# The first stage takes its 17 tiles in an interleaved order, and the tiles that are put aside share four slots

## The chip, the cores and the metric

One core of a Trainium2 chip runs the whole program. The time is the device time of one execution in microseconds; the median of several runs is compared.

## The reference, cut to what matters

One decoder layer over a prompt of 2064 rows (16 learned tokens and 2048 of the prompt) and eight single-row samples. Every row is normalised and projected through one combined matrix; an indexer scores the keys and each query keeps the best 256:

```python
xn = rmsnorm(xp, norm_g[l])
u, gc, q, k, v, ga, iq, ik, iw = project(xn, w_in[l])
...
s = jnp.einsum('bthd,bsd->bths', iq.astype(jnp.float32), ik_all.astype(jnp.float32))
score = jnp.einsum('bth,bths->bts', iw.astype(jnp.float32), jax.nn.relu(s))
_, idx = lax.top_k(score, topk)
...
xp = xp + merge(cy, gc, o, ga, w_out[l])
```

The outputs include k, v and ik of every row. Each matrix product of the prompt is made of three in the kernel, with each operand split into a high part (xh, wh) and a low part (xl, wl).

## The kernel before, in words

The rows are cut into 17 tiles of 128. Four stages follow one another, with a barrier between them. The change lies in the first, `project_norm_and_keys` (line 160), and in one helper table above it.

For each tile the first stage loads x (512 KB, into one of three places of `xst`), squares it on ACT (line 304), makes the reciprocal root on POOL (lines 294 and 296), scales it on DVE (line 337), transposes it on PE (line 369), and splits the result: ACT copies the high part into `mem.xh` (line 318), and DVE subtracts to get the low part in `mem.xl` (line 347). PE then projects k, v, ik and iw from it (24 matmuls, line 377), ACT copies them to `natst` (lines 322 to 325), and SP writes them out (lines 239 to 241). PE transposes ik (line 384) for the indexer.

The normalised tiles are needed again by the second stage. There are only nine slots for them on the chip, so tiles 0 to 7 (slots 0 to 7) are written to DRAM, 2 x 512 KB each (lines 260 and 261, here called the spill of a tile), and tiles 8 to 16 stay in slots 0 to 8. The second stage first works on tiles 8 to 16 and reads the eight others back later, by their tile numbers.

Each engine has a list of its own, written out by hand. On PE, ACT and DVE it is the list of jobs: for each i, "xT" of i + 1 (transpose and split), "nat" of i (projection), "ikT" of i - 1. On ACT, ahead of xT of i, comes the square of tile i + 2. DVE scales tile i + 1 ahead of the low part of i. SP, which issues all DMAs of the stage, runs through rounds i = 0 to 17, and in round i it issues:

```python
for i in range(NT + 1):
    if i < NT:
        if i + XS < NT:
            load_x(i + XS)
        if i < HALF:
            sp.wait_ge(dve_job, J.count(J.jobs.index(("xT", i)) + 1, ("xT", "ikT")))
            ...
        if i < LAST:
            load_pages(sp, range(2 * i, 2 * i + 2), ptab, t.cache_idx_k, "o s d -> (o s) d", ikp, pages_in)
    if i:
        write_natural(i - 1)
```

XS is 3. The load of x waits until the tile three places earlier is scaled; the spill waits for the low part of tile i; the two index pages of a round each need a register load from `ptab` (line 156) and a DMA (line 157); the three writes of tile i - 1 wait for its copy on ACT. SP goes strictly in this order, so that a wait holds back all that follows. Round 8 also loads eight small pieces of constants (line 270), and round 14 the first two weight chunks of the second stage (line 149). ACT waits for the spill of tile i - 8 before it overwrites its slot with tile i (line 317); the last tile has a free slot.

Of the kernel before, what the change touches and what calls it, by code (L numbers as in the profile page):

```python
# [6 lines left out]
f32 = mybir.dt.float32  # L7
# [3 lines left out]
ALU = mybir.AluOpType  # L11
ACT = mybir.ActivationFunctionType
# [7 lines left out]
P = 128  # L20
NT = -(-LP // P)
LAST = NT - 1
LREM = LP - LAST * P
SROW, NS = 32, 8
# [3 lines left out]
IH = 4  # L28
# [128 lines left out]
        eng.dma_start(dst[:, n, :], cache[0, bass.ds(v, 1)].rearrange(layout)).then_inc(pages_in, 16)  # L157


def project_norm_and_keys(nc, t, mem):  # L160


# [11 lines left out]
    with ExitStack() as ctx:  # L174
# [24 lines left out]
        nat_done = sem("nat_done")  # L199
        spill = [sem(f"x_spill{s}") for s in range(HALF)]  # L200
        nat_out = [sem(f"nat_out{s}") for s in range(2)]
        n_in = [len(tile_rows(i)) for i in range(NT)]
        ptab = sb("ptab", [1, NS * NPAGE], i32)
        ptab_in, pages_in = sem("ptab_in"), sem("pages_in")
        ikp = index_pages(mem)
# [6 lines left out]
            eng.wait_ge(nat_out[i % 2], 16 * n)  # L212

        def slot(i):
            return i if i < HALF else i - HALF
        block = ctx.enter_context(nc.Block())

        @block.sync
        def _(sp):
            def load_x(i):  # L220
                if i >= XS:
                    sp.wait_ge(xs_done, i - XS + 1)
                if i == LAST:
                    sp.wait_ge(zeroed, 1)
                for p0, n, what, r0 in tile_rows(i):
                    src = {"meta": t.meta_tokens, "x": t.x_prompt[0], "sample": t.x_sample[:, 0, :]}[what]
                    sp.dma_start(xst[p0:p0 + n, i % XS, :], src[r0:r0 + n, :]).then_inc(x_in[i % XS], 16)

            def write_natural(i):

                sp.wait_ge(nat_done, i + 1)
                n = natst[:, i % 2]
                for p0, rows, what in ([(0, P, "p")] if i < LAST else [(0, LREM, "p"), (SROW, NS, "s")]):
                    r = slice(i * P, i * P + rows)
                    ko = t.nk_p[0, 0, r] if what == "p" else t.nk_s[0, :, 0]
                    vo = t.nv_p[0, 0, r] if what == "p" else t.nv_s[0, :, 0]
                    io = t.nik_p[0, 0, r] if what == "p" else t.nik_s[0, :, 0]
                    q = slice(p0, p0 + rows)
                    sp.dma_start(ko.rearrange("t n d -> t (n d)"), n[q, 0:128]).then_inc(nat_out[i % 2], 16)
                    sp.dma_start(vo.rearrange("t n d -> t (n d)"), n[q, 128:256]).then_inc(nat_out[i % 2], 16)  # L240
                    sp.dma_start(io, n[q, 256:320]).then_inc(nat_out[i % 2], 16)
            load_x(0)
            sp.dma_start(gb[:, :], t.norm_g[0].unsqueeze(0).to_broadcast([128, D])).then_inc(g_in, 16)
            load_x(1)
            sp.dma_start(mem.cst[:, :], t.consts[:, 0:NCONST]).then_inc(c_in, 16)
            w3 = t.w_in[0].rearrange("(c p) n -> p c n", p=128)
            sp.dma_start(wn[:, :, 0:256], w3[:, :, OFF["k"]:OFF["k"] + 256]).then_inc(w_in_s, 16)
            sp.dma_start(wn[:, :, 256:NAT], w3[:, :, OFF["ik"]:OFF["ik"] + 68]).then_inc(w_in_s, 16)
            load_x(2)
            sp.dma_start(bcb[:, :], t.consts[0:32, NCONST:NCONST + BANDX]).then_inc(bias_in, 16)  # L250
            sp.dma_start(relb[:, :], t.rel_bias).then_inc(bias_in, 16)
            sp.dma_start(ptab[:, :], t.page_table.rearrange("b n -> (b n)").unsqueeze(0)).then_inc(ptab_in, 16)
            sp.wait_ge(ptab_in, 16)
            for i in range(NT + 1):
                if i < NT:
                    if i + XS < NT:
                        load_x(i + XS)
                    if i < HALF:
                        sp.wait_ge(dve_job, J.count(J.jobs.index(("xT", i)) + 1, ("xT", "ikT")))
                        sp.dma_start(t.d_xh[i], mem.xh[:, slot(i)].rearrange("p c t -> p (c t)").bitcast(f32)).then_inc(spill[i], 16)  # L260
                        sp.dma_start(t.d_xl[i], mem.xl[:, slot(i)].rearrange("p c t -> p (c t)").bitcast(f32)).then_inc(spill[i], 16)
                    if i < LAST:
                        load_pages(sp, range(2 * i, 2 * i + 2), ptab, t.cache_idx_k, "o s d -> (o s) d", ikp, pages_in)
                if i:
                    write_natural(i - 1)
                if i == HALF:

                    for dst, src in ((mem.lg, t.conv_ln_g), (mem.lb, t.conv_ln_b)):
                        for q in range(NQ):
                            sp.dma_start(dst[QA * q:QA * q + QA, :], src[0, P * q:P * q + P].rearrange("(g a) -> a g", a=QA),  # L270
                                         allow_slow_non_contiguous=True).then_inc(ln_in, 16)
                if i == LAST - 2:
                    for n in range(2):
                        load_weights(sp, t, mem, n)
            sp.wait_ge(ln_in, 16 * 2 * NQ)
            nat_written(sp, LAST)
            nat_written(sp, LAST - 1)
            sp.wait_ge(pages_in, 16 * NS * NPAGE)
            for s in range(HALF):
                sp.wait_ge(spill[s], 32)  # L280
# [17 lines left out]
        @block.scalar  # L298
        def _(act):
            def square(i):  # L300
                x_arrived(act, i)
                if i:
                    act.wait_ge(sq_done, i)
                nc.scalar.activation(sq[:, :], xst[:, i % XS, :], ACT.Square, accum_out=ssq[:, i:i + 1]).then_inc(sq_done, 1)
            square(0)
            square(1)
            act.wait_ge(w_in_s, 32)
            nc.scalar.activation(wnh[:, :, :], wn[:, :, :], ACT.Copy).then_inc(w_hi, 1)
            for n, (kind, i) in enumerate(J.jobs):
                if kind == "xT" and i + 2 < NT:  # L310
                    square(i + 2)
                act.wait_ge(pe_job, n + 1)
                u = psum[:, n % 4]
                if kind == "xT":
                    if i >= HALF:
                        if i < 2 * HALF:
                            act.wait_ge(spill[i - HALF], 32)
                    nc.scalar.activation(mem.xh[:, slot(i)].rearrange("p c t -> p (c t)"), u, ACT.Copy).then_inc(act_job, 1)
                elif kind == "nat":
                    if i >= 2:  # L320
                        nat_written(act, i - 2)
                    nc.scalar.activation(natst[:, i % 2, 0:256], u[:, 0:256], ACT.Copy)
                    nc.scalar.activation(natst[:, i % 2, 256:384].rearrange("p (a d) -> p a d", a=2),
                                         u[:, 256:320].unsqueeze(1).to_broadcast([128, 2, 64]), ACT.Copy).then_inc(nat_done, 1)
                    nc.scalar.activation(mem.iw[:, i], u[:, 320:324], ACT.Copy, scale=float(IH) ** -0.5).then_inc(act_job, 1)
                elif kind == "bias":
                    nc.scalar.activation(rrow[:, :], u[0:NH, 0:BANDX], ACT.Copy).then_inc(act_job, 1)
                else:
                    nc.scalar.activation(mem.ikh[:, i * P:(i + 1) * P], u[:, 0:128], ACT.Copy).then_inc(act_job, 1)

        @block.vector
        def _(dve):
# [7 lines left out]
            scale(0)  # L340
            for n, (kind, i) in enumerate(J.jobs):
                u = psum[:, n % 4]
                if kind == "xT":
                    if i + 1 < NT:
                        scale(i + 1)
                    dve.wait_ge(act_job, n + 1)
                    nc.vector.tensor_tensor(out=mem.xl[:, slot(i)].rearrange("p c t -> p (c t)"), in0=u,
                                            in1=mem.xh[:, slot(i)].rearrange("p c t -> p (c t)").bitcast(f32),
                                            op=ALU.subtract).then_inc(dve_job, 1)
                elif kind == "ikT":  # L350
                    dve.wait_ge(act_job, n + 1)
                    nc.vector.tensor_tensor(out=mem.ikl[:, i * P:(i + 1) * P], in0=u[:, 0:128],
                                            in1=mem.ikh[:, i * P:(i + 1) * P].bitcast(f32), op=ALU.subtract).then_inc(dve_job, 1)

        @block.tensor
        def _(pe):
            ident = part(mem.cst, "ident")
            for n, (kind, i) in enumerate(J.jobs):
# [11 lines left out]
                elif kind == "nat":  # L370
                    if i == 0:
                        pe.wait_ge(w_lo, 1)
                    pe.wait_ge(dve_job, J.count(J.jobs.index(("xT", i)) + 1, ("xT", "ikT")))
                    xh, xl = mem.xh[:, slot(i)], mem.xl[:, slot(i)]
                    for c in range(KC):
                        for k, (a, b) in enumerate(((xh, wnh), (xh, wnl), (xl, wnh))):
                            last = nc.tensor.matmul(u[:, 0:NAT], a[:, c, :], b[:, c, :], start=(c == 0 and k == 0),
# [1778 lines left out]
```

## Time and profile before

| what | value |
|---|---|
| runs | median 1750.65 us of 3 (1749.55 to 1751.58) |
| the profiled execution | 1748.58 us, span 1746.9 us |
| PE busy in the span | 1521.4 us (87%) |
| DVE | 1026.1 us (59%) |
| ACT | 722.6 us (41%) |
| POOL | 485.6 us (28%) |
| first stage | from the start to 122.35 us, where the second stage's first work starts |

Engines: PE is TensorE (PEld its weight loads), DVE VectorE, ACT ScalarE, POOL GpSimd, SP SyncE; SPq is SP's queue of issued DMAs. Times in the rows are microseconds from the start of the span. The stage is 7% of the span, so what it does is read from windows of its own time and not from the shares above.

### The profile page before, as it was taken

What the parts mean: (1) busy time and instruction counts of PE and PEld (TensorE: products, weight loads), DVE (VectorE), ACT (ScalarE), POOL (GpSimd) and SP (SyncE); (2) the same over time, 40 slices, a digit from 0 to 9 for tenths busy, and PEclk for the clock granted to TensorE, in tenths of its full rate; (3) what the DMA queues carried; (4) which work ended last, traced back from release to release, by engine and by line L of the source; (5) the groups of instructions that cost most, each with busy time, mean ns of one, the idle gap of its engine ahead of it and who ended that gap; (6) DMA issues with size and microseconds to landing.
All of it is one profiled execution on the core that took longest, in us unless ns stands there. A gap on an engine that the chain in (4) does not pass through costs nothing. (4 is left out here: it accounts for less than half of the span.)

```text
span 1746.9 us, 28490 instructions
## 1 busy us (share of the span) xinstructions
PE 1521.4 (87%) x10637; PEld 1298.9 (74%) x10637; DVE 1026.1 (59%) x2135; ACT 722.6 (41%) x1302; POOL 485.6 (28%) x334
## 2 busy tenths in 40 slices
PE   5698979979989799995489999999998887559998
PEld 5686979969989679995366777776666666448886
DVE  2333989879998798888224434455545555334332
ACT  4345413253222442221115555556556554355441
POOL 2120314613437412353321011002222233042321
PEclk9999989999999999998669999999999998779999
DMA  7632354112375402331571314411111122295542
GB/s 243 216 89 49 86 94 119 47 64 72 88 264 126 131 10 69 85 97 62 151 168 37 75 39 111 110 33 33 38 44 42 54 68 75 71 233 153 170 146 92
DMA packets 183118, 172.71 MB, mean 99 GB/s; under 512 B 58974, under 2 KB 155366, under 8 KB 182462
## 3 DMA queue, kind: packets, MB, share of 16 engines
q1 hardware_dynamic: 176974, 153.57, 31.9%
q10 hardware_dynamic: 4984, 15.24, 3.0%
q0 software_dynamic: 1024, 2.10, 0.4%
q8 instruction: 84, 1.38, 0.3%
q14 instruction: 52, 0.43, 0.1%
HBM read 109.35 MB, written 58.19 MB: 96 GB/s over the span
## 5 line engine op out<-in xcount | busy, mean ns | idle before, releaser
L769 PE MATMUL psum<-xh,wh 128*128 128x384 f32 (+1 forms) x1040 | 346.6, 333 | 20.1 <-ACT hst L715 11.1
L769 PE MATMUL psum<-xl,wh 128*128 128x384 f32 (+1 forms) x1040 | 343.4, 330 | 0.0
L769 PE MATMUL psum<-xh,wl 128*128 128x384 f32 (+1 forms) x1040 | 343.4, 330 | 0.0
L1359 ACT ACTIVATE pts<-psT 128x512 f32<-128x512 f32 (+1 forms) x302 | 167.1, 573 | 265.8 <-PE psT L1660 244.0
L769 PEld LDWEIGHTS psum<-xh,wh 128*128 128x128 f32 x1040 | 199.1, 191 | 23.2 <-ACT hst L715 14.2
L1539 DVE CUSTOM_DVE_ANT_0 L<-psU,mask 128x512 f32<-128x512 f32 (+3 forms) x260 | 143.5, 593 | 117.8 <-PE psU L1654 115.6
L1676 PE MATMUL psO<-pts,vs 128*64 128x128 f32 x2176 | 181.0, 287 | 27.0 <-ACT pts L1359 27.0
L769 PEld LDWEIGHTS psum<-xl,wh 128*128 128x128 f32 x1040 | 199.0, 191 | 0.0
L769 PEld LDWEIGHTS psum<-xh,wl 128*128 128x128 f32 x1040 | 198.8, 191 | 0.0
L900 DVE TENSOR_SCALAR_CACHE_REDUCE hit<-scores,T 128x1792 bf16<-128x1792 f32 (+8 forms) x120 | 184.6, 1538 | 11.7 <-issue 0.9
L1660 PE MATMUL psT<-cst,L 128*128 128x128 f32 x1105 | 172.4, 285 | 14.4 <-ACT L L1387 12.1
L1676 PEld LDWEIGHTS psO<-pts,vs 128*64 128x64 f32 x2176 | 113.6, 136 | 81.7 <-ACT pts L1359 56.5
L1387 ACT ACTIVATE L<-L,nm 128x1920 f32<-128x1920 f32 (+16 forms) x129 | 155.6, 1212 | 17.8 <-DVE nm L1544 17.7
L1660 PEld LDWEIGHTS psT<-cst,L 128*128 128x128 f32 x1105 | 121.3, 142 | 49.7 <-issue 20.9
L626 POOL TENSOR_TENSOR wl<-wst,wh 128x1024 fp32r<-128x1024 f32 x44 | 121.7, 2766 | 130.3 <-ACT wh L664 130.3
L1310 POOL TENSOR_SCALAR mask<-mask 128x2064 bf16<-128x2064 bf16 (+14 forms) x15 | 18.8, 1254 | 428.2 <-DMA mask<-d_mask 428.1
L1653 PE MATMUL psU<-kh,qt 128*128 128x512 f32 (+3 forms) x320 | 129.7, 409 | 2.7 <-DVE mx L1539 1.7
L1654 PE MATMUL psU<-kl,qt 128*128 128x512 f32 (+3 forms) x320 | 117.1, 376 | 0.0
L2045 PE MATMUL psO<-woh,fh 128*128 128x512 f32 x272 | 85.7, 397 | 31.3 <-POOL fl L1922 31.3
L725 ACT ACTIVATE r<-psum 128x1024 f32<-128x1024 f32 (+6 forms) x100 | 76.8, 807 | 42.4 <-DVE scores L849 25.6
L779 PE MATMUL psum<-ikh,iqs 128*128 128x512 f32 (+4 forms) x172 | 70.8, 413 | 26.1 <-ACT r L725 21.3
L1987 DVE TENSOR_TENSOR res<-psO,xr 128x1024 f32<-128x1024 f32 x17 | 20.8, 1225 | 121.0 <-PE psO L2045 121.0
(268 smaller groups left out, 2632.3 us busy)
## 6 DMA issues: line engine op xcount, KB each, us to landing
wst<-in_w_in SPq DMA_DIRECT2D x28, 512.0 KB
wst<-in_w_in SPq DMA_DIRECT2D x32, 256.0 KB
qt<-d_q SPq DMA_DIRECT2D x16, 512.0 KB, 3.9
xst<-in_x_prompt SPq DMA_DIRECT2D x15, 512.0 KB, 4.0
xr<-in_x_prompt SPq DMA_DIRECT2D x15, 512.0 KB, 4.7
out_y_prompt<-fin SPq DMA_DIRECT2D x15, 512.0 KB, 3.0
gate<-d_ga SPq DMA_DIRECT2D x17, 256.0 KB, 4.2
d_mix<-mix SPq DMA_DIRECT2D x17, 256.0 KB, 2.2
```

The source lines that it names most:

```text
L626: nc.gpsimd.tensor_tensor(out=wl[:, n % 2], in0=wst[:, n % 2], in1=wh[:, n % 2].bitcast(f32), op=ALU.subtract).then_inc(w_lo, 1)
L725: nc.scalar.activation(r[:, m % 2, 0:job[4]], u[:, 0:job[4]], ACT.Relu).then_inc(act_job, 1)
L769: last = nc.tensor.matmul(u[:, 0:k * P], a[:, w % 2, cc, :], x[:, s0:s0 + k, cc, :], start=(cc == 0 and e == 0), stop=(cc == KC - 1 and e ...
L900: V.tensor_scalar(hit[:, 0:width(i)], sc[c], at[:, c:c + 1] if len(at.shape) == 2 else at[:, c], 0.0, ALU.is_ge, ALU.add, accum_out=into[: ...
L1359: A.activation(out, src, ACT.Copy).then_inc(act_pt, 1)
L1387: A.activation(L[:, b, 0:width(i)], L[:, b, 0:width(i)], ACT.Exp, bias=nm[:, b:b + 1], accum_out=es[:, tile_no[i] % 2, j % GRP + 4 * side: ...
L1539: last = V.tensor_tensor_reduce(out=L[:, b, x0:x1], in0=u[:, x0 - a:x1 - a], in1=in1, scale=1.0, scalar=3 * NEG, op0=ALU.add, op1=ALU.max, ...
L1653: T.matmul(u[:, 0:k], q, kh[:, side, a:a + k], start=True, stop=False)
L1654: T.matmul(u[:, 0:k], q, kl[:, side, a:a + k], start=False, stop=True).then_inc(pe_u, 1)
L1660: last = T.transpose(pt[:, (side * k + e) * P:(side * k + e + 1) * P], L[:, (2 * p + side) % 4, (b + e) * P:(b + e + 1) * P], ident)
L1676: last = T.matmul(OT[64 * side:64 * side + 64, tile_no[i] % 2, j * P:(j + 1) * P], vs[0:rows, b + e, 64 * side:64 * side + 64], pts[0:rows ...
L2045: last = T.matmul(O[:, s, h * 512:(h + 1) * 512], a[:, n % FS, c, :], b[:, c, h * 512:(h + 1) * 512], start=(c == W_ORDER[0] and e == 0), ...
```

## The change

The first stage goes through the tiles in the order `FIRST_ORDER`: 0, 8, 1, 9, 2, 10, ... 7, 15, 16. The loops still count i from 0 to 16; i is now a place in this order, and the tile is `FIRST_ORDER[i]`. So the tiles that are put aside stand at the even places 0 to 14. Tiles 8 to 16 still end in slots 0 to 8, now each in its own slot from its turn on. Tiles 0 to 7 use slots 8, 7, 6, 5, 8, 6, 7, 8 (`ASIDE`), which later tiles take over: at places 8, 10, 11, 12, 13, 14, 15 and 16, ACT waits for the spill from place 0, 4, 6, 2, 10, 8, 12 and 14.

```diff
+FIRST_ORDER = [x for i in range(HALF) for x in (i, i + HALF)] + [LAST]
+ASIDE = [8, 7, 6, 5, 8, 6, 7, 8]
...
-        n_in = [len(tile_rows(i)) for i in range(NT)]
+        n_in = [len(tile_rows(i)) for i in FIRST_ORDER]
...
         def slot(i):
-            return i if i < HALF else i - HALF
+            return ASIDE[i] if i < HALF else i - HALF
+
+        def slot_emptied(eng, n):
+
+            i = FIRST_ORDER[n]
+            ahead = [x for x in FIRST_ORDER[:n] if x < HALF and slot(x) == slot(i)]
+            if ahead:
+                eng.wait_ge(spill[ahead[-1]], 32)
...
-                for p0, n, what, r0 in tile_rows(i):
+                for p0, n, what, r0 in tile_rows(FIRST_ORDER[i]):
...
-                    if i < HALF:
+                    tile = FIRST_ORDER[i]
+                    if tile < HALF:
                         sp.wait_ge(dve_job, J.count(J.jobs.index(("xT", i)) + 1, ("xT", "ikT")))
-                        sp.dma_start(t.d_xh[i], mem.xh[:, slot(i)].rearrange("p c t -> p (c t)").bitcast(f32)).then_inc(spill[i], 16)
-                        sp.dma_start(t.d_xl[i], mem.xl[:, slot(i)].rearrange("p c t -> p (c t)").bitcast(f32)).then_inc(spill[i], 16)
+                        sp.dma_start(t.d_xh[tile], mem.xh[:, slot(tile)].rearrange("p c t -> p (c t)").bitcast(f32)).then_inc(spill[tile], 16)
+                        sp.dma_start(t.d_xl[tile], mem.xl[:, slot(tile)].rearrange("p c t -> p (c t)").bitcast(f32)).then_inc(spill[tile], 16)
...
                 if kind == "xT":
-                    if i >= HALF:
-                        if i < 2 * HALF:
-                            act.wait_ge(spill[i - HALF], 32)
-                    nc.scalar.activation(mem.xh[:, slot(i)].rearrange("p c t -> p (c t)"), u, ACT.Copy).then_inc(act_job, 1)
+                    slot_emptied(act, i)
+                    nc.scalar.activation(mem.xh[:, slot(tile)].rearrange("p c t -> p (c t)"), u, ACT.Copy).then_inc(act_job, 1)
```

The other changed lines put `tile` in place of `i` where a tile's own rows or columns are addressed (the outputs, `mem.iw`, `mem.ikh`, `mem.ikl`).

The order of the jobs on PE, ACT and DVE is the same; which instructions wait, and what SP issues in a round, is not. On SP, the end of round 2 and the start of round 3 were (`natst` holds the projected tile, `ptab` the page table, `scores` is where the index pages land):

```order
L239 DMA out_nk_p<-natst 128x128 [waits nat_done]
L240 DMA out_nv_p<-natst 128x128
L241 DMA out_nik_p<-natst 128x64
L227 DMA xst<-in_x_prompt 128x1024 [waits xs_done]
L260 DMA d_xh<-xh 128x1024 [waits dve_job0]
L261 DMA d_xl<-xl 128x1024
L156 TENSOR_LOAD ptab
L156 ISA x2
L157 ISA
L157 DMA scores<-in_cache_idx_k 128x64
```

On SP, the same place is now:

```order
L253 DMA out_nk_p<-natst 128x128 [waits nat_done]
L254 DMA out_nv_p<-natst 128x128
L255 DMA out_nik_p<-natst 128x64
L240 DMA xst<-in_x_prompt 128x1024 [waits xs_done]
L156 TENSOR_LOAD ptab
L156 ISA x2
L157 ISA
L157 DMA scores<-in_cache_idx_k 128x64
```

The odd rounds have lost their spill and the wait ahead of it. The even rounds keep the piece of before, and go on with it up to round 14, where before the last spill stood in round 7.

On ACT, the end of the stage, from the split of the last tile but one to the copies of the last projection but one, was:

```order
L318 ACTIVATE xh<-psum 128x1024 [waits x_spill7,pe_job0]
L322 ACTIVATE natst<-psum 128x256 [waits nat_out0,pe_job0]
L323 ACTIVATE natst<-psum 128x128
L325 ACTIVATE iw<-psum 128x4
L329 ACTIVATE ikh<-psum 128x128 [waits pe_job0]
L318 ACTIVATE xh<-psum 128x1024 [waits pe_job0]
L322 ACTIVATE natst<-psum 128x256 [waits nat_out1,pe_job0]
```

On ACT, the same instructions are now:

```order
L332 ACTIVATE xh<-psum 128x1024 [waits x_spill6,pe_job0]
L336 ACTIVATE natst<-psum 128x256 [waits nat_out0,pe_job0]
L337 ACTIVATE natst<-psum 128x128
L339 ACTIVATE iw<-psum 128x4
L343 ACTIVATE ikh<-psum 128x128 [waits pe_job0]
L332 ACTIVATE xh<-psum 128x1024 [waits x_spill7,pe_job0]
L336 ACTIVATE natst<-psum 128x256 [waits nat_out1,pe_job0]
```

The last tile's high part has gained a wait, for the spill that SP issues two rounds earlier; before, the spills waited for were eight rounds old.

## Rows read from the trace of the kernel before

**Rows 1.** Windows: length, busy (count) of PE, PEld, DVE, ACT, POOL; clock, DMA share, GB/s
```profile
62.00:72.00 10.00, 6.72 (x49) 6.25 (x47) 2.62 (x3) 4.62 (x10) 1.30 (x4) 1.00 0.89 305
100.00:114.00 14.00, 14.00 (x103) 13.96 (x102) 7.57 (x9) 6.38 (x17) 0.99 (x2) 1.00 0.50 126
```

**Rows 2.** Waits of the first stage: engine, line, releaser: total us, times, longest
```profile
ACT sq L304 <- DMA xst<-in_x_prompt: 41.0, 14, 5.2
```

**Rows 3.** The same for SP's queue
```profile
SPq L260 <- DVE xl L347: 5.1, 3, 3.6
```

**Rows 4.** Timeline of SP, rounds 4 to 6: start, duration, line, DMA
```profile
44.77 0.43 SPq L227 DMA_DIRECT2D xst<-in_x_prompt  x1
45.24 0.43 SPq L260 DMA_DIRECT2D d_xh<-xh  x1
...
51.64 0.43 SPq L227 DMA_DIRECT2D xst<-in_x_prompt  x1
52.52 0.33 SPq L260 DMA_DIRECT2D d_xh<-xh  x1
...
58.61 0.43 SPq L227 DMA_DIRECT2D xst<-in_x_prompt  x1
```

**Rows 5.** Timeline of ACT and DVE in round 4: from the landing of x on
```profile
49.18 1.06 ACT L304 ACTIVATE sq<-xst 128x1024 f32<-128x1024 f32 x1 [4.85 <-DMA xst<-in_x_prompt]
...
50.24 1.00 ACT L318 ACTIVATE xh<-psum 128x1024 fp32r<-128x1024 f32 x1
...
51.27 1.22 DVE L347 TENSOR_TENSOR xl<-psum,xh 128x1024 fp32r<-128x1024 f32 x1 [4.96 <-ACT xh L318]
```

**Rows 6.** Timeline of SP, rounds without a spill: the end of round 8, round 9
```profile
76.52 1.88 SPq L270 DMA_DIRECT2D lg<-in_conv_ln_g  x4
...
80.35 0.43 SPq L227 DMA_DIRECT2D xst<-in_x_prompt  x1
...
84.45 0.43 SPq L227 DMA_DIRECT2D xst<-in_x_prompt  x1
```

**Rows 7.** Register loads of line 156, 34 to 60 us, then 72 to 84 us: min/median/max ns
```profile
L156 SPq TENSOR_LOAD <-ptab x7: 667/866/1521, 33.5 to 55.5; - x7
...
L156 SPq TENSOR_LOAD <-ptab x4: 265/268/272, 72.9 to 81.9; - x4
```

**Rows 8.** Landing of x, 36 to 72 us, then 72 to 100 us; of d_xl over the stage
```profile
DMA to landing us min/median/max: 4.0/4.3/4.4
...
DMA to landing us min/median/max: 3.6/3.8/4.0
...
DMA to landing us min/median/max: 3.6/5.9/7.2
```

**Rows 9.** Timeline of SP, rounds 0 to 2
```profile
18.64 0.35 SPq L260 DMA_DIRECT2D d_xh<-xh  x1
...
22.89 0.43 SPq L227 DMA_DIRECT2D xst<-in_x_prompt  x1
24.54 0.34 SPq L260 DMA_DIRECT2D d_xh<-xh  x1
...
29.61 0.43 SPq L227 DMA_DIRECT2D xst<-in_x_prompt  x1
30.30 0.33 SPq L260 DMA_DIRECT2D d_xh<-xh  x1
```

**Rows 10.** Timeline of SP at the end of the stage
```profile
98.40 0.36 SPq L227 DMA_DIRECT2D xst<-in_x_sample  x1
...
118.61 0.33 SPq L239 DMA_DIRECT2D out_nk_p<-natst  x1
```

**Rows 11.** Timeline of PE: transposes of tiles 15 and 16, then the transpose after nat 15
```profile
105.08 1.04 PE L369 MATMUL psum<-cst,xs 128*128 128x128 f32 x8
...
109.66 1.04 PE L369 MATMUL psum<-cst,xs 128*128 128x128 f32 x8
...
114.13 0.27 PE L384 MATMUL psum<-cst,natst 128*128 128x128 f32 x1
```

More of the change, by code:

```diff
@@ L232, in write_natural @@
                 n = natst[:, i % 2]
-                for p0, rows, what in ([(0, P, "p")] if i < LAST else [(0, LREM, "p"), (SROW, NS, "s")]):
-                    r = slice(i * P, i * P + rows)
+                tile = FIRST_ORDER[i]
+                for p0, rows, what in ([(0, P, "p")] if tile < LAST else [(0, LREM, "p"), (SROW, NS, "s")]):
+                    r = slice(tile * P, tile * P + rows)
                     ko = t.nk_p[0, 0, r] if what == "p" else t.nk_s[0, :, 0]
@@ L257, in _ @@
                         load_x(i + XS)
-                    if i < HALF:
+                    tile = FIRST_ORDER[i]
+                    if tile < HALF:
                         sp.wait_ge(dve_job, J.count(J.jobs.index(("xT", i)) + 1, ("xT", "ikT")))
-                        sp.dma_start(t.d_xh[i], mem.xh[:, slot(i)].rearrange("p c t -> p (c t)").bitcast(f32)).then_inc(spill[i], 16)
-                        sp.dma_start(t.d_xl[i], mem.xl[:, slot(i)].rearrange("p c t -> p (c t)").bitcast(f32)).then_inc(spill[i], 16)
+                        sp.dma_start(t.d_xh[tile], mem.xh[:, slot(tile)].rearrange("p c t -> p (c t)").bitcast(f32)).then_inc(spill[tile], 16)
+                        sp.dma_start(t.d_xl[tile], mem.xl[:, slot(tile)].rearrange("p c t -> p (c t)").bitcast(f32)).then_inc(spill[tile], 16)
                     if i < LAST:
@@ L313, in _ @@
                 u = psum[:, n % 4]
+                tile = FIRST_ORDER[i]
                 if kind == "xT":
-                    if i >= HALF:
-                        if i < 2 * HALF:
-                            act.wait_ge(spill[i - HALF], 32)
-                    nc.scalar.activation(mem.xh[:, slot(i)].rearrange("p c t -> p (c t)"), u, ACT.Copy).then_inc(act_job, 1)
+                    slot_emptied(act, i)
+                    nc.scalar.activation(mem.xh[:, slot(tile)].rearrange("p c t -> p (c t)"), u, ACT.Copy).then_inc(act_job, 1)
                 elif kind == "nat":
@@ L324, in _ @@
                                          u[:, 256:320].unsqueeze(1).to_broadcast([128, 2, 64]), ACT.Copy).then_inc(nat_done, 1)
-                    nc.scalar.activation(mem.iw[:, i], u[:, 320:324], ACT.Copy, scale=float(IH) ** -0.5).then_inc(act_job, 1)
+                    nc.scalar.activation(mem.iw[:, tile], u[:, 320:324], ACT.Copy, scale=float(IH) ** -0.5).then_inc(act_job, 1)
                 elif kind == "bias":
@@ L328, in _ @@
                 else:
-                    nc.scalar.activation(mem.ikh[:, i * P:(i + 1) * P], u[:, 0:128], ACT.Copy).then_inc(act_job, 1)
+                    nc.scalar.activation(mem.ikh[:, tile * P:(tile + 1) * P], u[:, 0:128], ACT.Copy).then_inc(act_job, 1)
         @block.vector
@@ L342, in _ @@
                 u = psum[:, n % 4]
+                tile = FIRST_ORDER[i]
                 if kind == "xT":
@@ L346, in _ @@
                     dve.wait_ge(act_job, n + 1)
-                    nc.vector.tensor_tensor(out=mem.xl[:, slot(i)].rearrange("p c t -> p (c t)"), in0=u,
-                                            in1=mem.xh[:, slot(i)].rearrange("p c t -> p (c t)").bitcast(f32),
+                    nc.vector.tensor_tensor(out=mem.xl[:, slot(tile)].rearrange("p c t -> p (c t)"), in0=u,
+                                            in1=mem.xh[:, slot(tile)].rearrange("p c t -> p (c t)").bitcast(f32),
                                             op=ALU.subtract).then_inc(dve_job, 1)
@@ L351, in _ @@
                     dve.wait_ge(act_job, n + 1)
-                    nc.vector.tensor_tensor(out=mem.ikl[:, i * P:(i + 1) * P], in0=u[:, 0:128],
-                                            in1=mem.ikh[:, i * P:(i + 1) * P].bitcast(f32), op=ALU.subtract).then_inc(dve_job, 1)
+                    nc.vector.tensor_tensor(out=mem.ikl[:, tile * P:(tile + 1) * P], in0=u[:, 0:128],
+                                            in1=mem.ikh[:, tile * P:(tile + 1) * P].bitcast(f32), op=ALU.subtract).then_inc(dve_job, 1)
         @block.tensor
@@ L373, in _ @@
                     pe.wait_ge(dve_job, J.count(J.jobs.index(("xT", i)) + 1, ("xT", "ikT")))
-                    xh, xl = mem.xh[:, slot(i)], mem.xl[:, slot(i)]
+                    s = slot(FIRST_ORDER[i])
+                    xh, xl = mem.xh[:, s], mem.xl[:, s]
                     for c in range(KC):
```

## The prediction

> **What bounds the stage now.** I read the windows of the first stage first, then its waits, then SP's timeline. The change touches the first 122 us alone: the nine slots hold the same tiles at its end, and the later stages are the same lists of instructions. So only the length of this stage can move the end, and what it gains or loses passes through whole. In the windows, PE is busy 6.72 of 10 us while tiles are put aside, and all of 14 us once they are no longer [rows 1]. The granted clock is 1.00 (2.4 GHz) in both, so PE waits there, and is not slower. The DMAs stand at a share of 0.89 and 305 GB/s in the first of the two windows. From this one might say that the transfers are the limit of the first half, and that spreading the spills is a gain.
>
> The waits say something else about order. ACT waits 41.0 us, in 14 pieces, for x to land [rows 2]; SP itself waits for the low part that it is to spill only 5.1 us, in 3 pieces [rows 3]. So x is late because SP issues it late. SP's timeline shows rounds of 6.9 to 7.0 us (44.77 to 51.64 to 58.61) while there are spills [rows 4], and of 4.10 us without (80.35 to 84.45) [rows 6]. Part of the difference is the register load ahead of a page: 667 to 1521 ns beside the spills, 265 to 272 ns without them [rows 7].
>
> There is a second chain hidden below that. The spill of round i needs the low part of tile i; on ACT the high part of tile i stands behind the square of tile i + 2; and x of tile i + 2 is issued at the start of round i - 1. Rows 5 show it once: x, issued at 44.77, lands at 49.18, its square and the high part follow at once, and the low part ends at 52.49 (51.27 + 1.22). SP issues the spill at 52.52 [rows 4], 7.75 us after the load of the round before. With two equal rounds of about 7 us SP gets there by itself at about 7.4 us, so that this chain costs next to nothing now. It is what the change meets.
>
> **The sum, part by part.** I call a(i) the time at which SP issues x in round i, and s(i) that of its spill.
>
> From s(i) to the next a: 52.52 to 58.61 is 6.09 us, 45.24 to 51.64 is 6.40 [rows 4]. These spills stand within 0.9 us of an x load. In round 1 the load was 1.65 us ahead of the spill, and 24.54 to 29.61 is 5.07 [rows 9]. After the change the distance is 3 us, which only round 0 has (and more); there 18.64 to 22.89 is 4.25 without the three writes. An issue takes SP 0.47 us (44.77 to 45.24) [rows 4], so the floor is a quiet round with two spill issues in place of the x issue: 4.10 - 0.47 + 0.94 = 4.57, if no register load is slow. I take 5.6, between round 1 and the crowded rounds, and keep 4.57 and 6.40.
>
> From a(i - 1) to s(i): landing plus 3.35 us (52.52 - 49.18). The landing is 4.3 us (4.0 to 4.4) where spills follow close behind, 3.8 (3.6 to 4.0) where none do [rows 8]. After the change x of an odd round goes out with no spill behind it, and the last spill is over 5 us old. I take 3.8, which makes 7.15, and keep 6.95 and 7.75.
>
> An odd round without a spill lets SP reach the spill of the even round after 4.10 + 0.47 = 4.57 us, but the low part is there after 7.15: **SP now waits 2.6 us in front of every second spill**, and pages, the three writes of the tile before and the next x stand behind it. A pair of rounds takes 7.15 + 5.6 = 12.75 us. PE's own pace, 4.58 us a tile (105.08 to 109.66) [rows 11], is 9.16 for a pair and lies below it. Before, a pair cost 14 us in the first half, but only about 9.2 in the second. The slow pairs now reach to the end.
>
> s(2) stays at 30.30: before, SP already waited for this low part (0.69 us after the load at 29.61) [rows 9]. Then
> a(3) = 30.30 + 5.6 = 35.9;
> a(13) = 35.9 + 5 x 12.75 + 3.83 = 103.5. The 3.83 us (76.52 to 80.35) are the small constants at the end of round 8 [rows 6]; before, they lay partly beside PE's work too, and I leave them whole, as they follow a waited-for spill;
> s(14) = 103.5 + 7.15 + 0.4 = 111.05. The 0.4 is the second load of the last tile (98.40, 0.36 us) [rows 10].
> PE can start the projection of place 14 when that low part is there, at 111.0. Before it started when the transposes of tile 15 were done, at 105.08 + 1.04 = 106.12 [rows 11]. From there on PE goes without a gap: before, 12.5 us to the last copy (SP writes it at 118.61) [rows 10], and the same after. **Shift: 4.9 us.**
>
> The added wait on ACT: the last projection would start 8.2 us after that of place 14 (106.12 to 114.3) [rows 11], at 119.2, and needs the last high and low part, 1.0 and 1.2 us [rows 5], so that the high part must start by 116.9. The second spill goes out at 111.5. At the median landing of 5.9 us it is there at 117.4, 0.5 us too late; at 3.6 it is hidden, at 7.2 it costs 1.8 [rows 8]. I take 0.5. The other reuse waits are for spills four rounds or more old, and cost nothing, as over 20 us lie between. The weight chunks of round 14 now go out at about 117, some 10 us before the second stage wants them, and an x of the same size lands in 4.
>
> Sum: 4.9 + 0.5 = 5.4 us longer. The profiled execution (1748.58 us) would take 1754.0; the median of the runs shown lies 2.07 us higher, and so does the forecast, **1756.0 us**.
>
> **Rivals.** *Quick rounds.* With the cheapest prices, 6.95 and 4.57, a pair is 11.5 and a(13) is 34.9 + 57.6 + 3.8 = 96.2, place 14 starts at 103.6: 2.5 us shorter, 1748.1. With round 1's 5.07 it is 0.6 us longer, 1751.3. Between them and a pair of 12.4 the change is within 0.2% (3.5 us), which is about what a measurement of this kernel can tell from none. For it speaks that the traffic is thinner now; against it that the first pages still come right after two spills, where each crowded round had slow loads.
>
> *Rounds as dear as before.* With 7.75 and 6.40 a pair is 14.15: a(13) = 36.7 + 70.8 + 3.8 = 111.3, place 14 starts at 119.4, 13.3 us later, 1764. For it speaks that this is what rounds 4 and 6 did; against it that no spill stands behind the x that is waited for.
>
> *Spread traffic wins.* If the DMA load of the first half is what sets the pace, thinner traffic lets x land so early that SP never stands before a spill, and PE's pace sets the rounds. Then pairs are 9.16 us, a(13) = 35.9 + 45.8 + 3.8 = 85.5, place 14 starts at 93.1, 13 us earlier: about 1738. This decides once a pair is below 11.8 (no change) or 11.3 (clearly faster), which needs a landing below 2.9 or 2.3 us at my other prices. The share of 0.89 [rows 1] speaks for it; that x never landed in under 3.6 us even with half the traffic [rows 8] speaks against it. The Trainium skill, page "DMA: Bandwidth & Descriptors", section "Issuing engines are not separate DMA queues", is on this rival's side: it calls the time to initiate a DMA on the sequencer usually small relative to the DMA itself. The trace does not agree here: SP's rounds are full of issue and register loads, with 5.1 us of waits [rows 3]. The same page's section "Where 436 GB/s comes from" gives about 358 GB/s as the HBM side's limit; by that the 1.8 MB of a spilling round (512 KB of x, 1 MB of spill, 160 KB of outputs, 64 KB of pages) would need an estimated 5.0 us, which leaves the 7 us rounds to something else than bandwidth.
>
> **Chances.** Forecast case, a pair of 12.4 to 13.5: 0.45. Quick rounds, within 0.2%: 0.31. As dear as before, over 13.5: 0.16. Spread traffic: 0.08. Hence faster 0.08, same 0.31, slower 0.61. The range goes from the floor of the quick rounds, 1748, to the dear ones, 1764, and leaves out the last rival and the ends beyond.
>
> **What would show it.** Right: SP waits for the low part in seven even rounds, about 2.6 us each and 15 to 20 us in all, against 5.1; loads of x alternate in distance, about 4.1 and 8.6 us; the second stage starts near 128 us; PE is idle in pairs up to 110 us, where now it is full. Wrong: rounds of equal length near 4.6 us (spread traffic), or SP's wait absent; a second stage that starts at 122 (quick rounds). The wait for the last spill should show on ACT for at most 2 us.

## The result, and the profile after

The changed kernel takes 1755.39 us (median of 15 runs, 1752.03 to 1761.95), the kernel before 1750.5 us beside it (15 runs, 1748.03 to 1754.16). The ratio is 1.0026, with a 95% interval of 1.0016 to 1.0035: slower by about a quarter of a per cent. The profiled execution has a span of 1752.9 us, 6.0 more than before. Of these, 4.8 lie in the first stage, as the first instruction of the second stage on ACT shows (122.35 us before):

```profile
127.14 2.00 ACT L680 ACTIVATE wh<-wst 128x1024 fp32r<-128x1024 f32 x2 [3.00 <-PEq L180]
```

The other 1.2 us lie in stages that have not changed, and are less than the spread of single runs.

The waits of SP in the first stage (line, releaser, total us, times, longest) answer to [rows 3]:

```profile
SPq L275 <- DVE ikl L367: 14.2, 6, 2.8
SPq L275 <- DVE xl L362: 5.3, 2, 3.8
```

Both rows are the wait for the low part ahead of a spill. The first names the short instruction on DVE that starts at about the same time as the low part ends; the spill at 67.66 below stands at the end of the low part (66.40 + 1.23), not at that of the other one. Together they are 19.5 us in 8 waits. Counted in the same way, the wait before was not 5.1 but 6.4 us in 5 waits, as it has a second row too, which the prediction left out:

```profile
SPq L260 <- DVE ikl L352: 1.3, 2, 0.6
```

The longest wait is that of round 0, 3.8 us now and 3.6 before. The seven even rounds behind it have 15.7 us, 2.2 us each. SP's timeline over a pair of rounds and a half (start, duration, line, DMA) answers to [rows 4]:

```profile
60.64 0.43 SPq L240 DMA_DIRECT2D xst<-in_x_prompt  x1
61.82 1.46 SPq L157 DMA_DIRECT2D scores<-in_cache_idx_k  x2
...
64.76 0.43 SPq L240 DMA_DIRECT2D xst<-in_x_prompt  x1
67.66 0.33 SPq L275 DMA_DIRECT2D d_xh<-xh  x1
68.02 0.43 SPq L276 DMA_DIRECT2D d_xl<-xl  x1
69.79 1.87 SPq L157 DMA_DIRECT2D scores<-in_cache_idx_k  x2
...
89.68 0.48 SPq L240 DMA_DIRECT2D xst<-in_x_prompt  x1
...
96.75 0.33 SPq L275 DMA_DIRECT2D d_xh<-xh  x1
...
102.28 1.18 SPq L240 DMA_DIRECT2D xst<-in_x_prompt  x1
```

From 60.64 the next load is 4.12 us away; then SP stands still from 65.2 to 67.66 until the low part is there, 7.02 us after the first load. The pair from 89.68 to 102.28 has 12.60 us: 7.07 to the spill, 5.53 from there. The loads of x land in 3.7 us (median of 28 to 104 us), where before they took 4.3 beside the spills:

```profile
DMA to landing us min/median/max: 3.7/3.7/4.2
```

PE at the end of the stage (start, duration, line; idle time and releaser in brackets) answers to [rows 11]; the windows under it show length, busy time of PE, PEld, DVE, ACT and POOL, then granted clock, DMA share and GB/s:

```profile
105.21 1.04 PE L384 MATMUL psum<-cst,xs 128*128 128x128 f32 x8
109.15 0.39 PE L393 MATMUL psum<-wnh,xh 128*128 128x324 f32 x1 [2.90 <-DVE xl L362]
...
109.79 0.47 PE L393 MATMUL psum<-wnh,xh 128*128 128x324 f32 x1
110.06 0.47 PE L393 MATMUL psum<-wnl,xh 128*128 128x324 f32 x1
...
114.35 0.27 PE L400 MATMUL psum<-cst,natst 128*128 128x128 f32 x1
```
```profile
62.00:72.00 10.00, 8.26 (x60) 8.03 (x59) 4.65 (x5) 5.16 (x12) 1.48 (x4) 1.00 0.65 231
100.00:114.00 14.00, 11.10 (x69) 10.87 (x68) 6.10 (x7) 4.43 (x12) 0.74 (x2) 0.88 0.39 126
```

The first window has gained against [rows 1] (PE 8.26 of 10 us instead of 6.72), the second has lost (11.10 of 14 instead of 14.00). The traffic is in fact smoother, 231 GB/s against 305. The first half of the stage, which has fewer spills now, did get shorter: the load of round 8 goes out at 64.76 and not at 72.44. The slow pairs of the second half lose this again and more: the load of round 13 goes out at 102.28 and not at 97.99. The matmuls from 109.79 to 112.76 follow one another every 0.27 us, and every 0.15 us from 112.99 on: the granted clock was at the lower of its two levels (1.2 GHz; the window from 109 to 115 has 0.72 in the mean), behind 2.90 us without work.

### The profile page after: what moved, and what is told of

It is laid out like the page before. It is cut to its first block and busy times, and to the rows that moved or that the text cites. A ratio compares the mean times of both kernels' runs of the same rounds, so it can differ in the third digit from the quotient of the medians.

```text
span 1752.9 us, 28490 instructions
## 1 busy us (share of the span) xinstructions
PE 1528.9 (87%) x10637; PEld 1305.9 (75%) x10637; DVE 1032.3 (59%) x2135; ACT 722.9 (41%) x1302; POOL 482.9 (28%) x334
## 5 line engine op out<-in xcount | busy, mean ns | idle before, releaser
L785 PE MATMUL psum<-xh,wh 128*128 128x384 f32 (+1 forms) x1040 | 346.8, 334 | 20.1 <-ACT hst L731 11.2
L1676 PE MATMUL psT<-cst,L 128*128 128x128 f32 x1105 | 171.5, 284 | 13.2 <-ACT L L1403 12.1
L795 PE MATMUL psum<-ikh,iqs 128*128 128x512 f32 (+4 forms) x172 | 72.5, 423 | 24.6 <-ACT r L741 19.5
```

Of the source, the lines that this page charges most:

```text
L785: last = nc.tensor.matmul(u[:, 0:k * P], a[:, w % 2, cc, :], x[:, s0:s0 + k, cc, :], start=(cc == 0 and e == 0), stop=(cc == KC - 1 and e ...
L1676: last = T.transpose(pt[:, (side * k + e) * P:(side * k + e + 1) * P], L[:, (2 * p + side) % 4, (b + e) * P:(b + e + 1) * P], ident)
```

## The experiments

Each is timed against the kernel before on the same chip. "Stage end" is the start of the second stage's first instruction on ACT (before 122.35, changed 127.14 us). A page is one of the 32 index pages. A stage end comes from one profile. How far it can move with nothing changed in what comes before it, the fillers of experiments 5 and 7 show: their load of round 13 went out at 103.91 and 107.02 us, against 102.28 in the changed kernel, although the added work had not begun by then. So a difference of stage ends of up to 5 us is not certain by itself. The ratios of the timed runs stand beside it; the changed kernel's is 1.0026.

**1. The square behind the high part, in the changed kernel.** On ACT:

```diff
-                if kind == "xT" and i + 2 < NT:
-                    square(i + 2)
...
                     nc.scalar.activation(mem.xh[:, slot(tile)].rearrange("p c t -> p (c t)"), u, ACT.Copy).then_inc(act_job, 1)
+                    if i + 2 < NT:
+                        square(i + 2)
```

> The changed kernel; on ACT the square of tile place i + 2 stands behind the high part of place i instead of ahead of it, so that a spill no longer waits for the landing of the x load of the round before. Theory (SP stands before every second spill until that x has landed; profile after: 19.5 us in 8 waits, pairs of 12.6 us): the waits fall below 4 us, a pair of rounds takes SP's own time, 4.1 + 0.47 + 5.5 = 10.1 us, the place 14 starts some 13 us earlier, time about 1741 us. Rival 1 (traffic or SP's issue sets the pair and the wait only fills a gap): pairs stay near 12.6 us, 1755. Rival 2 (the waits for emptied slots cost): the same 12.6 us, with ACT waiting for spills.

Measured: 1747.24 us against 1749.79, ratio 0.9988 (0.9976 to 1.0001); stage end 120.29, 6.9 us earlier than in the changed kernel. Of the 19.5 us of waits for low parts 3.9 are left:

```profile
SPq L275 <- DVE xl L362: 3.6, 2, 2.8
SPq L275 <- DVE ikl L367: 0.3, 1, 0.3
```

So the wait held the pairs at 12.6 us, and undoing it takes back the whole loss (the timed runs, from 1.0026 to 0.9988, say 0.4%, some 7 us). But the pairs came to 11.1 to 12.0 us, not 10.1, since a spill now follows the x load at once and the crowded price is back:

```profile
53.15 0.44 SPq L240 DMA_DIRECT2D xst<-in_x_prompt  x1
53.64 0.43 SPq L275 DMA_DIRECT2D d_xh<-xh  x1
54.11 0.43 SPq L276 DMA_DIRECT2D d_xl<-xl  x1
56.64 1.94 SPq L157 DMA_DIRECT2D scores<-in_cache_idx_k  x2
...
60.08 0.45 SPq L240 DMA_DIRECT2D xst<-in_x_prompt  x1
```

From the spill to the next load are 6.44 us (6.4 to 6.7 in all five pairs), as in round 4 of before (6.40) [rows 4]; I had put in 5.5.

**2. The same in the kernel before.**

> The kernel before with the same exchange on ACT. Theory: SP is already full in the first half (5.1 us of waits), and the chain was just covered by two rounds of 7 us, so the exchange is worth 0 to 4 us here, 1747 to 1750. If the exchange gained as much here as in the changed kernel (over 10 us), the chain was not made worse by the interleaving, and the theory falls.

Measured: 1747.98 us against 1749.79, ratio 0.9986 (0.9973 to 0.9999), stage end 122.12, 0.2 us earlier. The chain costs 0.2 us of the stage (0.14% of the time) in the old order, and 6.9 us (0.4%) in the new one: it is the interleaving that exposes it.

**3. The spill at the end of SP's round.** The two DMAs and their wait stand behind `write_natural(i - 1)` instead of ahead of the pages.

> The changed kernel; SP issues the spill at the end of its round, behind the pages and the three writes; nothing else moves. Theory: the low part is there when SP comes to it (4.1 + 4.1 = 8.2 us after the x load of the round before, 7.1 needed), so the waits vanish, a pair takes 9.2 us of issue and 1 to 1.5 us of slow register loads, about 10.5, time about 1743 us. Rival 1: pairs stay at 12.6, 1755.

Measured: 1746.6 us against 1749.79, ratio 0.9977 (0.9966 to 0.9988); stage end 117.23, 9.9 us earlier than the changed kernel. SP waits once for a low part, for 1.5 us. Pairs have 10.3 to 10.7 us up to round 7, and 9.4 to 12.1 behind it (constants taken off). The instructions and the bytes are the same; only the place of the spill and its wait in SP's list is different.

**4. Pages in the odd rounds.**

```diff
-                    if i < LAST:
-                        load_pages(sp, range(2 * i, 2 * i + 2), ptab, t.cache_idx_k, "o s d -> (o s) d", ikp, pages_in)
+                    if i < LAST and i % 2:
+                        load_pages(sp, range(2 * i - 2, 2 * i + 2), ptab, t.cache_idx_k, "o s d -> (o s) d", ikp, pages_in)
```

> The changed kernel; the four pages of two rounds are loaded in the odd round, none in the even one, so that SP does them where it would stand still, and the slow register loads behind a spill go. Theory: from the x load of the odd round to the spill 7.1 us as now, from the spill to the next x load 0.94 + 1.47 = 2.4 to 3 us instead of 5.5, a pair 9.6 to 10.2 us, 1742 us. If bytes in flight set the pair, it stays at 12.6 us.

Measured: 1748.2 us against 1749.79, ratio 0.9985 (0.9972 to 0.9998); stage end 121.65, 5.5 us earlier than the changed kernel. Pairs of 11.2 to 12.4 us, and 10.9 us of waits for low parts instead of 19.5: the direction is right, the size half of what I expected. The timeline shows where the rest went:

```profile
66.92 0.33 SPq L275 DMA_DIRECT2D d_xh<-xh  x1
67.28 0.43 SPq L276 DMA_DIRECT2D d_xl<-xl  x1
67.76 1.13 SPq L253 DMA_DIRECT2D out_nk_p<-natst  x1
68.93 1.18 SPq L254 DMA_DIRECT2D out_nv_p<-natst  x1
70.16 0.60 SPq L255 DMA_DIRECT2D out_nik_p<-natst  x1
```

The register loads are now short (21 from 36 to 99 us, median 268 ns), but the small writes that took their place behind the spill are issued in 1.13 and 1.18 us instead of 0.43. So it is not the register load as such: what SP does next behind two issues of 512 KB is slow. What holds it up no run here shows.

**5 and 7. Does the idle time cost the clock?** Both add 24 transposes of the identity to PE ahead of the projection of place 14. The first try put them behind PE's wait for a place in PSUM, which is itself a wait for the low part, so that they delayed the projection. The second writes them to a free part of PSUM, ahead of all waits:

```diff
+                if (kind, i) == ("nat", 14):
+                    for _ in range(24):
+                        nc.tensor.transpose(psum[:, (n - 2) % 4, 512:640], ident, ident)
                 if n >= 4:
                     pe.wait_ge(act_job, n - 3)
```

> The changed kernel; PE does 24 more transposes of the identity (about 2.7 us, into a place that the following matmul overwrites) where it stands idle before the projection of place 14. In the profile of the changed kernel that projection took 5.2 us instead of 3.6, at a granted clock below 1 behind the idle time. Theory: with PE busy the clock stays, the projection takes 3.6 to 3.8 us and the second stage starts 1.3 to 1.6 us earlier (125.6 to 125.9). If the clock had another cause, the projection stays at 5.2 us. Neither shows in the time for sure (0.1%).

> The changed kernel; 24 transposes of the identity (2.8 us) on PE ahead of the projection of place 14, now into a part of PSUM that is free, so that they fill the 2.9 us in which PE waits for the low part. (The try before put them behind that wait: the projection then took 3.7 us, not 5.2, but began 2.6 us late.) Theory: the projection begins at 109.1 as in the changed kernel and takes 3.6 to 3.8 us, the second stage starts at 125.4 to 125.9 instead of 127.1, time 1.5 us less or, with the noise of the later stages, the same.

Measured: the first 1765.67 us against 1752.48, ratio 1.0064 (1.0041 to 1.0086), stage end 129.53; the second 1758.86 against 1751.96, ratio 1.0043 (1.0029 to 1.0057), stage end 131.08. In the profile of the second:

```profile
109.14 2.78 PE L377 MATMUL psum<-cst 128*128 128x128 f32 x24
113.18 0.39 PE L396 MATMUL psum<-wnh,xh 128*128 128x324 f32 x1 [1.26 <-DVE xl L362]
113.40 0.31 PE L396 MATMUL psum<-wnl,xh 128*128 128x324 f32 x1
...
116.84 0.27 PE L403 MATMUL psum<-cst,natst 128*128 128x128 f32 x1
```

With the gap filled but for 1.26 us, the projection goes at the upper level (a matmul every 0.15 us) and takes 3.66 us (113.18 to 116.84) instead of 5.20 (109.15 to 114.35). So the lower clock cost 1.5 us, and with less idle time it did not come. That the idle time alone brings it is not shown, and the kernel before speaks against it. Its PE waited for a low part seven times, up to 3.1 us, and the granted clock was 1.00 in all windows of these waits:

```profile
PE psum L377 <- DVE xl L347: 15.9, 7, 3.1
48.00:62.00 14.00, 9.53 (x67) 9.09 (x66) 5.23 (x6) 5.47 (x14) 1.48 (x4) 1.00 0.79 260
86.00:100.00 14.00, 12.41 (x88) 12.41 (x89) 8.53 (x10) 8.64 (x22) 3.36 (x8) 1.00 0.56 166
```

In the changed kernel the clock fell behind 2.78 us (at 55.30), 6.92 us (at 84.08) and 2.90 us (at 109.15). Before, it stayed behind 2.79 us (at 52.64) and 3.10 us (at 87.59). Of two gaps of the same length one is followed by the lower clock and the other is not, so the length of one gap doesn't tell. The first two falls of the changed kernel lie within pairs in which PE waits anyway.

The forecast of the stage end missed: the low part of place 14 came 4 us later than in the changed kernel's profile (SP's spill at 113.06 instead of 109.03), because the pairs of rounds before it were longer, before the added work had run at all. One profile of each doesn't say whether that is spread or an effect of the longer program. The timed runs of the second are as slow as its stage says (0.43% is 7.5 us above before, the stage 8.7 us). Those of the first are not (0.64% is 11.2 us, the stage 7.2); in its profile the rest lies behind the first stage. Both stay open.

**6. Pages on POOL's queue, in the order of before.** The two pages of round i are loaded by POOL behind its reciprocal root of tile i.

> The kernel before, with the index pages loaded from POOL's queue instead of SP's. Theory (SP's issue sets the 7 us rounds of the first half, not the transfers): a round needs 2.9 us of SP, then the chain of load, square, split and spill sets (7.75 + 2.4) / 2 = 5.1 us a round, or the bytes 5.5; place 8 is reached some 12 us earlier, time about 1739 us. If the transfers set the pace (share 0.89, 305 GB/s), rounds stay near 7 us and the time at 1750.

Measured: 1746.16 us against 1752.48, ratio 0.9956 (0.9939 to 0.9973); stage end 118.40. From round 2 on, rounds of the first half have 5.1 to 6.5 us instead of 7, with 22.31 of 24 us of PE work (36 to 60 us) at 304 GB/s. The transfers were not what made 7 us rounds. The stage gained 4 us and not 12. Of the missing 8 us, 5.6 are a late start: POOL, busy with pages, makes the low part of the weights late (shown under 8 and 9), and SP's round 2 starts at 35.22 instead of 29.61.

**8 and 9. Both edits, in either order of tiles.**

> The changed kernel with both, pages on POOL's queue and the square behind the high part. Theory: neither SP nor the chain holds PE up, PE's pace of 4.6 us a tile sets the stage, which ends some 18 us earlier than in the kernel before, 1733 us. If the mean traffic (1.25 MB a tile at 4.6 us, 270 GB/s) is too much, 1738 or more.

> The kernel before with both. Theory: now the bytes of the first half (1.8 MB a round) bound its rounds at 5.5 to 6 us, then PE's 4.6; the stage ends about 11 us earlier than in the kernel before, 1739 us. So the interleaving would win 4 to 8 us once SP and the chain are out of the way. If the transfers of the first half are not a bound at 4.6 us a round either, both orders end alike, at 1733.

Measured: 1738.1 us against 1752.48 with the interleaved order, ratio 0.9909 (0.9888 to 0.9929), stage end 112.99; 1741.49 with the order of before, ratio 0.9935 (0.9914 to 0.9956), stage end 113.44. The intervals overlap, and the stages end within half a microsecond. (The profiled execution of the first took 1747.66 us, the slowest of its five, mostly behind this stage.) The late start is on POOL in both (here with the interleaved order); the subtraction at line 301 began at 15.4 before:

```profile
20.50 0.54 POOL L157 DMA_DIRECT2D scores<-in_cache_idx_k  x1 [0.55 <-issue]
21.06 5.67 POOL L301 TENSOR_TENSOR wnl<-wn,wnh 128x2592 fp32r<-128x2592 f32 x1
```

**10 and 11. The same with POOL's pages from its fourth round on.**

```diff
+                if i == 3:
+                    pool.wait_ge(ptab_in, 16)
+                if 3 <= i < 14:
+                    load_pages(pool, range(3 * i - 9, min(3 * i - 6, NS * NPAGE)), ptab, t.cache_idx_k, "o s d -> (o s) d", ikp, pages_in)
```

> As the changed kernel with the pages on POOL's queue and the square behind the high part, but POOL begins with the pages in its fourth round only, three a round. With pages from the first round on, POOL reached its subtraction of the weights' low part at 21.1 us instead of 15.4, and the first projection was 6 us late. Theory: that start comes back, PE goes at 4.6 us a tile from the third tile on, the second stage starts at 105 to 107 us, time 1733 to 1735.

> The order and slots of before with the same three edits. In the version without the late start PE was full from 36 to 60 us at a DMA share of 0.97 and 339 GB/s. Theory now (the transfers never bound the first half, SP's issue did): the second stage starts at the same time as with the interleaved order, within 1 us, and the times agree within 0.2%. If spread transfers matter once the rest is out of the way, this one is 3 us or more slower.

Measured: 1736.06 us against 1751.96 with the interleaved order, ratio 0.9910 (0.9891 to 0.9928), stage end 108.98; 1735.33 with the order of before, ratio 0.9906 (0.9890 to 0.9923), stage end 106.27. The ratios agree to 0.04%, each known to about 0.2%, and the stage of the interleaved order ends 2.7 us later in its profile, not earlier. Windows of the second one:

```profile
36.00:60.00 24.00, 24.00 (x174) 23.81 (x172) 12.23 (x15) 13.03 (x33) 10.15 (x22) 1.00 0.98 338
60.00:84.00 24.00, 23.61 (x164) 22.44 (x163) 14.06 (x16) 14.80 (x37) 12.43 (x25) 1.00 0.73 208
```

PE is full in the half with the spills, at a DMA share of 0.98. So with SP's list short and the chain cut, the uneven traffic of the old order fits, and spreading it is worth nothing that these runs can tell. This version beats both kernels, the one before by 0.9%.

**12. Only the pages on POOL (from its fourth round), in the changed kernel.**

> The changed kernel with the pages on POOL's queue from its fourth round on, and nothing else. Theory: SP needs 2.4 to 2.5 us from a spill to the next x load, 7.05 us from there to the next spill remain, a pair takes 9.5 us and still contains the wait (SP waits for low parts over 25 us in all), the second stage starts at 107 to 110 us, time 1736 to 1739. So most of the loss is SP's issue behind the wait; the exchange of square and high part adds only what is left down to PE's 9.2 us.

Measured: 1747.01 us against 1751.96, ratio 0.9982 (0.9966 to 0.9998), stage end 117.90. The wait for the low part grew to 27.4 us, as expected, since SP had less to do beside it. The rest missed: a pair took 10.8 to 12.0 us and not 9.5, the stage ended 8 us late and the time is 8 us above the forecast:

```profile
53.68 0.33 SPq L275 DMA_DIRECT2D d_xh<-xh  x1
54.05 0.43 SPq L276 DMA_DIRECT2D d_xl<-xl  x1
54.53 0.79 SPq L253 DMA_DIRECT2D out_nk_p<-natst  x1
55.35 1.76 SPq L254 DMA_DIRECT2D out_nv_p<-natst  x1
57.16 0.43 SPq L255 DMA_DIRECT2D out_nik_p<-natst  x1
```

As in 4, what comes behind the spill is slow (3.95 us here to the next load, not 2.4), and the loads took longer, 4.6 us to land instead of 3.7:

```profile
DMA to landing us min/median/max: 3.9/4.6/5.1
```

Against 10, which differs by the exchange on ACT alone, this one ends its stage 8.9 us later and is 10.95 us slower. The pages alone had gained 9.2 us of stage (127.14 to 117.90). So SP's issue and the chain count about alike; the expectation that issue is most of the loss was wrong.

## Why the prediction was right

The forecast was 1756.0 us, 5.4 more than before in the profile's terms; measured were 4.9 more in the medians (1755.39 - 1750.5). The steps against the profile after:

| step | predicted | measured |
|---|---|---|
| spill of round 2 | 30.30 | 30.30 |
| load of round 3 | 35.9 | 35.41 |
| from x load to the spill of the next round | 7.15 us | 7.02 to 7.12 in four pairs, 7.53 and 6.75 in one each |
| from the spill to the next x load | 5.6 us | 5.46 to 5.72 in five rounds, 5.11 and 5.12 in two |
| a pair of rounds | 12.75 us | 12.61 in the mean of five (102.28 - 35.41 - 3.80, by 5) |
| spill of round 14 | 111.05 | 109.03 |
| start of the projection of place 14 | 111.0 | 109.15, 3.0 later than before |
| from there to the last copy's write | 12.5 us | 14.26 (to 123.41) |
| wait for the last spill | 0.5 us | 0 |
| the stage in all | +5.4 us | +4.8 us |
| SP's waits for low parts | 15 to 20 us | 19.5 us |

The mechanism is shown, not only argued: the wait moved onto SP's path, with nearly the size that was worked out (2.2 us in each of seven even rounds, forecast 2.6), and cutting it down or filling it by three unlike edits (the order on ACT, the place of the spill in SP's list, the pages beside the wait) brought the stage back by 6.9, 9.9 and 5.5 us. All three have ratios of 0.9977 to 0.9988 in the timed runs, where the changed kernel has 1.0026. The exchange on ACT that frees the new order does next to nothing for the old.

That the total came so close is in part luck: two terms were missed, and cancelled. The start of place 14 came 1.9 us too late in my sum (0.5 us up to round 3, 0.7 over five pairs, 0.8 in the last one, whose x took 6.75 us to the spill instead of 7.55), and the tail was 1.8 us too short: "from there on PE goes without a gap: before, 12.5 us, and the same after" left out that PE would run the first projection at the lower clock (1.5 us; the other 0.2 is that the projection of before began at 105.87, ahead of the end of the transposes). The rows of before could not have told: there PE kept its clock behind waits as long. The 5.6 us from a spill to the next load was a choice between 5.07 and 6.40 and no result of a mechanism; 5.11 to 5.72 were measured. The wait for the last spill was the third, 0.5 us: ACT took the last high part at 115.53, when PE's transposes were ready, and not when a spill landed. The DMAs of d_xl now land in 4.0 us (median) and not in the 5.9 of the crowded first half. The reuse waits were misread, at no cost: those at places 13 and 15 are for spills three rounds old, not four or more, and 11.5 to 14.6 us lie between, not over 20. No low part of a spill took more than 6.1 us to land, and ACT waits for no spill in the stage.

```profile
115.53 1.02 ACT L332 ACTIVATE xh<-psum 128x1024 fp32r<-128x1024 f32 x1 [0.19 <-PE psum L384]
```

Of the rivals, spread traffic falls with the windows of experiment 11: even a share of 0.98 leaves PE full, so the 0.89 of [rows 1] was no bound. Its ground was that issue is usually small beside the transfer (the Trainium skill, "DMA: Bandwidth & Descriptors", "Issuing engines are not separate DMA queues"). For a single load of x the trace agrees, 0.43 us of issue against 3.7 us to land. But the issues add up on one queue: eight DMAs and two register loads fill a round of 7 us. Experiments 3 and 6 change only where in the list or by whom DMAs are issued, and not one byte, and shortened the stages of the kernels they start from by 9.9 and 4.0 us. The quick rounds' prices did not come, with 5.5 us behind most spills; the dear rounds' price came in experiment 1, where spill and load stand together again, and in two rounds of experiment 7 (6.26 and 7.22 us).

## What to carry to other kernels

Before spreading a burst over a loop, write down what the issuing queue waits for in each turn: a wait that is covered while every turn is long becomes exposed when every second turn is short, and all that stands behind it in that queue comes late with it. A high DMA share beside an idle engine is no proof of a bandwidth bound; look whether the queue that issues the transfers has idle time, and if it has none, move issues to an engine that has, but not ahead of work that the start depends on. Small gains can add up, and a side effect can hide one: in the old order the queue gave 0.44%, the chain 0.14%, both together 0.65%, about their sum, and 0.94% once POOL's pages no longer made the start late.

## What was not expected of the hardware

- Behind two issues of 512 KB on SP the next instructions are slow, whether they are register loads or writes. In rounds 2 to 7 of before the first register load takes 1.3 to 1.6 us there instead of 0.27 (0.9 us in the changed kernel, where the spill stands apart from the x load). Where it was moved away, two or three of the small writes take 0.8 to 1.8 us each to issue instead of 0.43 (experiments 4 and 12). Moving the pages away gains 0.2 to 1.9 us a pair and not the 3 that were expected.
- Behind 2.90 us without work PE's granted clock was at the lower level for most of the next projection (24 matmuls in 5.20 us). With 24 small transposes in the gap, and 1.26 us left idle, it was not (3.66 us). But behind 2.79 and 3.10 us without work in the kernel before it was not either, and behind 2.19 us (at 70.19 in experiment 7) it was.
- Landing times of x rose to 6.2 us (6.1 to 6.4) at 338 GB/s in experiment 11 while PE had no idle time from 36 to 60 us. My reading is that three places of x cover them once no spill waits for the newest; no run tests it.
